# Six modulation parts summed over the partitions by single-pass products of a rounded high part and a low part

## The reference, cut to what matters

```python
mod = c @ w_ada[l] + b_ada[l]
shift_m, scale_m, gate_m, shift_f, scale_f, gate_f = jnp.split(mod, 6, axis=-1)
h = modulate(rms_norm(x, g_pre_mix[l]), shift_m, scale_m)      # then projections, attention, mLSTM, mix
x = x + gate_m[:, None, :] * rms_norm(mix, g_post_mix[l])
h2 = modulate(rms_norm(x, g_pre_ffn[l]), shift_f, scale_f)
ff = (jax.nn.silu(h2 @ w_ffn_gate[l]) * (h2 @ w_ffn_up[l])) @ w_ffn_down[l]
x = x + gate_f[:, None, :] * rms_norm(ff, g_post_ffn[l])
```

## Time and profile before

| | |
|---|---|
| median of 3 runs | 795.09 us (794.2 to 799.14) |
| the profiled execution | 793.67 us, span of the profile 791.8 us |
| TensorE clock granted | 0.994 of full speed over the span |
| TensorE busy (PE) / weight loads (PEld) | 761.5 us (96%) / 675.7 us (85%) |
| VectorE busy (DVE) | 615.4 us (78%) |
| ScalarE busy (ACT) | 375.9 us (47%) |
| HBM read | 171.60 MB, 218 GB/s over the span |

### The profile page before, as it was taken

How to read it: one execution, slowest core, us unless ns; L and a number is a source line. 1 busy time by engine, 2 the same in 40 slices (tenths; PEclk the granted TensorE clock), 3 DMA queues, 4 the chain that set the end, 5 groups by cost and what they waited for, 6 DMA issues and landing times.

```text
span 791.8 us, 15369 instructions
## 1 busy us (share of the span) xinstructions
PE 761.5 (96%) x6380; PEld 675.7 (85%) x6380; DVE 615.4 (78%) x813; ACT 375.9 (47%) x553; POOL 41.4 (5%) x61
## 2 busy tenths in 40 slices
PE   4999999989999999999999999999899999999996
PEld 3798899989768999998876987989675999999874
DVE  5869989988978888887868899786697788556457
ACT  3367743744354544453345696432225444454340
POOL 0124000000000000000001000040010000000000
PEclk9999999999999999999999999999999999999998
DMA  9997867764668899988992644301673399666621
GB/s 342 319 318 223 296 213 221 246 227 129 199 230 309 291 351 322 343 303 302 371 334 61 204 128 138 108 4 46 202 236 105 114 315 319 187 189 199 195 83 53
DMA packets 98067, 173.65 MB, mean 219 GB/s; under 512 B 7767, under 2 KB 55230, under 8 KB 97998
## 3 DMA queue, kind: packets, MB, share of 16 engines
q1 hardware_dynamic: 95678, 166.62, 62.8%
q0 software_dynamic: 1872, 5.86, 2.6%
q10 hardware_dynamic: 448, 0.19, 0.1%
HBM read 171.60 MB, written 1.05 MB: 218 GB/s over the span
## 4 chain that ended last, share of the span: by engine, by line
PE 71%; DVE 20%; DMA 4%; issue 3%; ACT 2%; DVEq 0%; SPq 0%; ACTq 0%
PE bank L2246 12%; PE bank L2247 12%; PE bank L2248 12%; PE bank L2302 5%; PE bank L2566 5%; PE bank L2567 5%; PE bank L2568 5%; DVE wlo L498 3%; DVE acc L525 3%; DMA raw<-in_w_ada 2%; PE bank L2722 2%; DVE arena L1365 1%; PE bank L2223 1%; PE bank L2164 1%; PE bank L2225 1%
## 5 line engine op out<-in xcount | busy, mean ns | idle before, releaser
L498 DVE TENSOR_TENSOR wlo<-raw,whi 128x1024 fp32r<-128x1024 f32 (+1 forms) x200 | 239.7, 1213 | 83.2 <-ACT whi L735 80.0
L735 ACT ACTIVATE whi<-raw 128x1024 fp32r<-128x1024 f32 (+1 forms) x200 | 207.2, 1051 | 200.6 <-PE bank L2248 76.2
L2246 PE MATMUL bank<-hh,whi 128*128 128x256 f32 x952 | 267.2, 281 | 0.5 <-DVE wlo L498 0.4
L2247 PE MATMUL bank<-hl,whi 128*128 128x256 f32 x952 | 263.7, 277 | 0.0
L2248 PE MATMUL bank<-hh,wlo 128*128 128x256 f32 x952 | 263.7, 277 | 0.0
L2246 PEld LDWEIGHTS bank<-hh,whi 128*128 128x128 f32 x952 | 178.8, 188 | 3.8 <-issue 2.8
L2247 PEld LDWEIGHTS bank<-hl,whi 128*128 128x128 f32 x952 | 178.8, 188 | 1.2 <-issue 1.2
L2248 PEld LDWEIGHTS bank<-hh,wlo 128*128 128x128 f32 x952 | 179.3, 188 | 0.0
L2566 PE MATMUL bank<-whi,ffh 128*128 128x512 f32 x168 | 65.7, 391 | 0.9 <-DVE wlo L498 0.9
L2567 PE MATMUL bank<-wlo,ffh 128*128 128x512 f32 x168 | 65.4, 389 | 0.0
L2568 PE MATMUL bank<-whi,ffl 128*128 128x512 f32 x168 | 65.4, 389 | 0.0
(11 more groups left out here) (464 smaller groups left out, 1097.4 us busy)
## 6 DMA issues: line engine op xcount, KB each, us to landing
raw<-in_w_ada SPq DMA_DIRECT2D x96, 512.0 KB, 5.3
raw<-in_w_in SPq DMA_DIRECT2D x50, 512.0 KB, 5.0
raw<-in_w_ffn_in SPq DMA_DIRECT2D x80, 256.0 KB, 4.2
raw<-in_w_ffn_down SPq DMA_DIRECT2D x22, 512.0 KB, 5.3
raw<-in_w_ffn_out SPq DMA_DIRECT2D x22, 512.0 KB, 4.2
raw<-in_w_ffn_gate SPq DMA_DIRECT2D x40, 256.0 KB, 4.4
raw<-in_w_ffn_up SPq DMA_DIRECT2D x40, 256.0 KB, 5.7
raw<-in_w_out SPq DMA_DIRECT2D x16, 512.0 KB, 4.1
```

The source lines that it names most:

```text
L498: eng.tensor_tensor(lo[:, 0:nk * width], raw[:, b % RAW, 0:nk * width], hi[:, 0:nk * width].bitcast(fp), ALU.subtract)\
L735: act.activation(weight_place(g)[0][:, 0:nk * width], raw[:, b % RAW, 0:nk * width], ACT.Copy)\
L2246: mm(o, wh[:, k, c], xh[:, kk_, :], start=first, stop=False)
L2247: mm(o, wh[:, k, c], xl[:, kk_, :], start=False, stop=False)
```

## The change

For parts 5, 6, 7, 8, 9 and 11, VectorE adds two instructions behind the last accumulation: it rounds the accumulator to fp32r (`sum_hi`) and subtracts that from the accumulator into `sum_lo` (in place of the accumulator, or in its old room). With parts 5 and 11 it also writes a rounded 128x128 matrix of ones, with part 5 one of 128x32 too. The products then take the high and the low part one after the other, each as a single-pass product. A gate is four products of 512 columns in place of two float32 ones; a part in columns is sixteen products of 32 columns in place of eight float32 ones. TensorE waits on the semaphore `sum_split` instead of on the last accumulation. VectorE waits for its own last accumulation before the high part, for the high part before the low part, and for earlier sums on TensorE (`piece_done`) before it writes over the room of their accumulators. Parts 0 to 4 and 10 stay as they were, as do the orders of ScalarE, GpSimd and SyncE.

```diff
+        SPLIT_SUMS = {5: 4, 6: 6, 7: 8, 8: 10, 9: 12, 11: 15}
+
+        def part_split(d):
+
+            sums = 2 * FT * S + 2048
+            at = {5: sums + 4 * D, 6: ARENA - 2048, 7: ARENA - 1024, 8: sums + D, 9: sums, 11: sums + 4 * D}[d]
+            own = pos_acc[0] if d in GATES else sums + D * (d - 6)
+            one = rounded("ones128", ARENA - P, [P]) if d in GATES else rounded("ones32", sums + 5 * D, [SUM_N])
+            return one[:, :], rounded(f"sum_hi{d}", at, [D])[:, :], rounded(f"sum_lo{d}", own, [D])[:, :]
...
                     eng.scalar_tensor_tensor(to, x, by, to, ALU.mult, ALU.add)\
                        .then_inc(sem(f"{me}_blocks"), 1)
+                    if k == 7 and d in SPLIT_SUMS:
+
+                        one, hi, lo = part_split(d)
+                        if d in GATES:
+                            eng.tensor_scalar(one, C("ones"), 1.0, None, ALU.mult).then_inc(sem("sum_split"), 1)
+                        if d == 5:
+                            eng.tensor_scalar(part_split(6)[0], C("ones")[:, 0:SUM_N], 1.0, None, ALU.mult)\
+                               .then_inc(sem("sum_split"), 1)
+                        eng.wait_ge(sem(f"{me}_blocks"), count)
+                        if 6 <= d <= 9:
+                            eng.wait_ge(sem("piece_done"), {6: 6, 7: 6, 8: 8, 9: 7}[d])
+                        eng.tensor_scalar(hi, to, 1.0, None, ALU.mult).then_inc(sem("sum_split"), 1)
+                        eng.wait_ge(sem("sum_split"), SPLIT_SUMS[d] - 1)
+                        eng.tensor_tensor(lo, to, hi.bitcast(fp), ALU.subtract).then_inc(sem("sum_split"), 1)
...
+                if d in SPLIT_SUMS:
+
+                    one, hi, lo = part_split(d)
+                    pe.wait_ge(sem("sum_split"), SPLIT_SUMS[d])
+                    if d in GATES:
+                        for h in range(2):
+                            c = slice(512 * h, 512 * h + 512)
+                            mm(bank[at + h][:, :], one, hi[:, c], start=True, stop=False)
+                            last = mm(bank[at + h][:, :], one, lo[:, c], start=False, stop=True)
+                    else:
+                        x = 8 * SUM_N * (d == 9)
+                        for t in range(8):
+                            o, c = bank[at][:, x + SUM_N * t:x + SUM_N * t + SUM_N], slice(t * P, t * P + P)
+                            mm(o, hi[:, c], one, start=True, stop=False)
+                            last = mm(o, lo[:, c], one, start=False, stop=True)
+                    last.then_inc(sem("piece_done"), 1)
+                    return
```

More of the change, by code:

```diff
@@ L205, in build @@
         wlo = ctx.enter_context(nc.sbuf_tensor("wlo", [P, HL, SLOT], fr))
+        acc_at = -(-nc.sbuf_base // 32) * 32
         acc = sb("acc", [P, D])
+        pos_acc = [(acc_at - arena_at) // 4]
         xt = sb("xt", [P, MT, D])
```

## The result

The changed kernel's median is 801.04 us (797.68 to 809.33, 16 runs); the kernel before beside it had 795.5 us (16 runs). The ratio is **1.0093**, 95% interval [1.0075, 1.011], some 7.4 us where the forecast had 1.5; the medians lie 5.5 us apart, the means 6.3 us. Its profiled execution took 801.85 us, span 800.0 us. Four later runs, two of late32 and two of hold, were over 1.5% longer than the fastest of their kernel and are left out of all means.

A forecast was written before the change was run, and what follows sets the result against it. TensorE was taken as the bound, waiting where VectorE's added work delays low parts of weights. Parts 5, 6, 7 and 11 summed to 1.0 + 1.2 + 0.1 - 0.8 = 1.5 us slower: median 796.6 us, range 794.5 to 798.5 us.

The forecast's parts named there:

- The gates: TensorE, parts 5 and 11: four single-pass products, 0.92 us, replace two float32 ones, 1.72 us; 0.8 us saved each.
- the narrow products: TensorE, parts 6 to 9: still sixteen records, no saving; a rival had them faster by 5 us at most, chance 0.12.
- the high part: VectorE, each split part: 0.75 us for the rounding; a rival had 0.5 us more in each pair, chance 0.13.
- the low part: VectorE, each split part: 1.23 us for the subtraction, 1.14 us up to the next start.
- the cover of parts 8 and 9: Behind parts 8 and 9: room of 4.5 us covers 2.2 us, and 3.0 us covers 2.0 us; nothing lost.
- part 11: At gf6: the low part comes at 666.6, TensorE at 667.1; it fits by 0.5 us, 0.8 us kept.
- the waits: TensorE waits for low parts of weights: 1.75 us at ff3, 1.2 us at ff6, none or a tiny one at ff9.
- the term of part 6: At ff6: TensorE ready at 301.5, first low part at 302.7, so 1.2 us more.
- The sum: Whole kernel: 1.0 + 1.2 + 0.1 - 0.8 = 1.5 us slower, for parts 5, 6, 7 and 11.

The follow-up runs named there:

- late32: The changed kernel with the 128x32 ones written at part 6 instead of part 5; ratio 1.0116 to the kernel before.
- hold: The changed kernel with GpSimd's first masked product held until VectorE's (L2001) is done; ratio 1.0053 to the kernel before.
- gates: Only parts 5 and 11 split, parts 6 to 9 summed as in the kernel before; ratio 1.0039 to it.
- shift4: The changed kernel with four VectorE instructions that only count up a finished semaphore, ahead of the gram step; ratio 1.007 to the kernel before.
- sixf: The changed kernel with four counting VectorE instructions ahead of the gram step and an added float32 product inside ff3, ff6 and ff9; ratio 1.0042 to the kernel before.
- gate11: Only part 11 split, the other five parts summed as in the kernel before; ratio 0.9977 to it.
- nops4: The changed kernel with four empty VectorE instructions that leave nothing in the program, so in effect a repeat; ratio 1.0092 to the kernel before.
- before16s: The kernel before with sixteen VectorE instructions that only count up a finished semaphore, ahead of the gram step; ratio 1.0043 to the kernel before.
- again: The changed kernel once more, no edit; ratio 1.0094 to the kernel before.
- draws: The kernel before with one float32 product of 128 columns added behind each of items ff2 to ff9; ratio 1.0019 to the kernel before.
- not5: Parts 6, 7, 8, 9 and 11 split, part 5 summed in float32 as in the kernel before; ratio 1.0052 to it.

## Why the forecast was wrong

Stage by stage, in us, each trace less that of before, the clock's falls ahead of the end (1.7 us for each 3.4 us at half clock) taken out:

| stage | after | gates | shift4 | sixf | gate11 | forecast for after |
|---|---|---|---|---|---|---|
| to ff2 | -0.5 | -0.3 | +0.2 | -0.7 | -0.2 | 0 |
| ff2 to ff3 (gate 5, wait) | +1.2 | +0.4 | +1.0 | +0.8 | 0.0 | +1.0 |
| ff3 to ff10 | +3.1 | +3.1 | +1.0 | +2.1 | 0.0 | +1.3 |
| parts 6 to 9, down projection | 0.0 | -0.1 | -0.1 | +0.1 | 0.0 | 0 |
| k, r, v, gram step | +1.8 | -0.5 | -0.6 | -0.9 | -0.3 | 0 |
| gf0 to gate 11 and end | -0.8 | -0.8 | -0.5 | -0.8 | -0.4 | -0.8 |

**What held.** The gates (0.92 us for 1.72, L2187 and L2188), the narrow products (109 ns, no gain), the high part (684 to 695 ns) and the low part (1225 ns), the cover of parts 8 and 9, and part 11. Where neither of the two new places strikes, in shift4, the waits stand where the forecast had them, two thirds to three quarters as long; TensorE's waits there (line, releaser: us in all, times, longest):

```profile
PE bank L2291 <- DVE wlo L510: 2.1, 2, 1.3
```

1.3 us at ff3 (forecast 1.75) and 0.8 at ff6 (forecast 1.2), and 0.3 us more by ff9. Over the traces of the six-part kernels the wait at ff3 was 0.5 to 1.5 us, and from the gate to ff3's start it was 0.2 to 1.2 us longer than before, against 1.0 in the forecast. sixf, as the mean of its runs, ends at +1.2 ± 1.2 us where the forecast's sum is 1.5 and the three products add 0.7.

**The step that failed** is in the term of part 6, "are eight items, 10.88 us each, so ff6 started at 267.84 + 32.65 = 300.5, now at 301.5 if all is ready". It took the length of an item from the trace of before as fixed. An item takes 10.88 or 11.3 us. Behind the float32 gate product, which the change removes, ff3 began at the shorter one in eight traces of nine; behind the four single-pass products in four of eleven. The slow pace costs up to 3.4 us; from shift4 to sixf, 2.4 us plus the 0.7 us of the products, with an error of over 1 us. It can also hide waits, as VectorE gains 0.42 us per item: that would be why after has no wait at ff6 where the forecast had 1.2 us, though nops4, slow up to there too, still waited 0.57.

**The sum** failed as well: it ended with part 11 and had nothing for code that the change doesn't touch. The sixteen VectorE records more put the late count, 831, on the one instruction that starts together with GpSimd's; before, it fell on one behind running work, 9 us later. That costs 2.5 us by shift4, 2.6 by before16s. The trace of before had the ground for a rival in it: two engines start a masked product in the same 10 ns, and VectorE takes 1.23 us for the first and 3.18 us for the next of the same shape.

Together: 1.5 (terms) + 2.5 (collision) + some 2 to 3 (pace) make the +6.0 to +6.2 us of the full-clock times of again and nops4; the share of the pace is what is left over, within the errors above, and no experiment gives it by itself in this kernel. The 6.3 us between the means of after and before have 0.4 to 0.9 us of clock in them besides, which took 6.7 us from after's runs and 5.8 to 6.3 from those of before in the later groups. Why TensorE has two paces, and what of a float32 product ends the slow one, stays open: no record shows the cause, and draws shows that such a product doesn't always end it.

## What to carry to other kernels

Count the instructions of a saturated stretch, not its busy time: at 100% busy and full clock an engine can be 4% slower. Before adding instructions to an engine's stream, look for places far behind where VectorE and GpSimd start in the same instant, since some tenths of a us swap their order there. And judge a small change by many runs of the whole kernel, as effects of its parts don't add up: alone, these came to 2.4 us of 6.0.

## What the hardware showed unasked

- TensorE's single-pass 256-column products run 113.3 or 117.8 ns apart, for tens of us, at the full clock. Behind the float32 products that I added the pace was 113 in thirteen of fourteen places, in five of them after 118 ahead and in eight after 113; the other is the one ahead of gate 5 in draws, with 113 ahead and 118 behind.
- A VectorE record at a fixed count, number 831, starts 0.35 us later than usual if it stands behind a semaphore record, in eleven traces of eleven and with two different instructions there.
- A masked product of VectorE, 1.23 us in first place, takes 3.11 us when GpSimd's 2.38 us began 0.35 us earlier; the other way round GpSimd's pair takes 6.80 in place of 5.71 us.
- Ahead of its end, a traced execution has one to four falls of the clock to half (1.2 GHz), for 3.4 or 6.8 us each. Some stand where TensorE is busy throughout (at 361 us in not5, in the narrow products, 13.0 us of 13), others where it has gaps (at 175 us in before, 12.5 us of 15).
